# Residual, squares and norm statistic inside the first output projection, one expert's loads moved behind them, and three smaller moves, in a two-block network on one core

## The reference

```python
# first block
x = x + g1 * (jnp.concatenate([ssd_x, attn_x], axis=-1) @ w_out)
h2 = rms_norm(x, norm2) * (1 + sc2) + sh2
moe_x = hier_moe(h2, w_group, b_group, w_expert, b_expert, w_gate, w_up, w_down)
x = rms_norm(x + g2 * moe_x, norm_final)
# second block, two layers; xc (the context) goes the same way
merged = (g_f * (y_f @ w_br_fourier) + g_d * (o_d @ w_br_diff)
          + g_g * (o_g @ w_br_gqa) + g_c * (y_c @ w_br_conv))     # g_*: sigmoid gates
x = x + gx1 * rms_norm(merged @ w_out, g_post_mix)
hm = rms_norm(x, g_pre_mlp) * (1 + cx2) + sx2
x = x + gx2 * rms_norm(jnp.square(jax.nn.relu(hm @ w_ff1)) @ w_ff2, g_post_mlp)
```

## Time and profile before

| | before |
|---|---|
| median of 3 runs | 3932.5 us (3932.43 to 3933.34) |
| the profiled execution, its own time | 3933.81 us |
| its span in the trace | 3931.9 us |
| TensorE busy | 3729.5 us (95%) |
| VectorE busy | 1867.9 us (48%) |
| GpSimd busy | 1031.1 us (26%) |
| ScalarE busy | 832.4 us (21%) |
| mean granted clock of TensorE | 0.985 |
| DMA | 475.13 MB, mean 121 GB/s |

### The profile page before, as it was taken

One profiled execution on the slowest core, in us unless ns is written; L12 is line 12 of the kernel. 1 busy time (PEld: TensorE's weight loads), 2 busy tenths in 40 slices (PEclk: granted clock), 3 DMA queues, 4 the chain that ended last, 5 costly groups with the idle time before them and its releaser, 6 DMA issues. The chain is left out here.

```text
span 3931.9 us, 47902 instructions
## 1 busy us (share of the span) xinstructions
PE 3729.5 (95%) x18308; PEld 2555.2 (65%) x18308; DVE 1867.9 (48%) x3512; ACT 832.4 (21%) x1688; POOL 1031.1 (26%) x888
## 2 busy tenths in 40 slices
PE   7988789999999999999998999999999999989998
PEld 6776545555565586555554555555887767778887
DVE  4466323222412376886545666656125655143445
ACT  3125211111201264111213000002124611220001
POOL 2331100000023202132332222232142034443443
PEclk9999899999999999999999999999999999999999
DMA  5410599999411100222221222221120022212221
GB/s 213 187 71 1 220 351 395 394 395 398 195 59 54 38 1 17 93 89 77 102 79 54 108 107 107 107 87 53 49 76 23 12 75 81 81 65 97 86 86 54
DMA packets 72302, 475.13 MB, mean 121 GB/s; under 512 B 8272, under 2 KB 9680, under 8 KB 18960
## 3 DMA queue, kind: packets, MB, share of 16 engines
q1 hardware_dynamic: 68864, 461.35, 31.3%
q0 software_dynamic: 2640, 8.65, 0.8%
q10 hardware_dynamic: 576, 2.10, 0.1%
HBM read 467.87 MB, written 4.19 MB: 120 GB/s over the span
## 5 line engine op out<-in xcount | busy, mean ns | idle before, releaser
L1030 PE MATMUL ps<-projected,weight_ring 128*128 128x384 f32 (+1 forms) x672 | 245.8, 521 | 0.0
L3598 PE MATMUL ps<-projected,weight_ring 128*128 128x384 f32 (+1 forms) x768 | 223.0, 434 | 1.2 <-DVE mlp_u L3797 0.7
L2478 DVE SCALAR_TENSOR_TENSOR sb_x_all<-ps,sb_modulation_ada,sb_x_all 128x512 f32<-128x512 f32 x144 | 106.5, 750 | 244.6 <-PE ps L2303 215.0
L1030 PEld LDWEIGHTS ps<-projected,weight_ring 128*128 128x128 f32 x672 | 127.7, 190 | 106.1 <-issue 45.9
L3598 PEld LDWEIGHTS ps<-projected,weight_ring 128*128 128x128 f32 x768 | 144.8, 190 | 62.5 <-issue 3.0
L3598 PE MATMUL ps<-projected,mlp_weight_sums 128*128 128x384 f32 x480 | 165.8, 488 | 0.0
L1398 DVE TENSOR_REDUCE attention_shift<-ps 128x1 f32<-128x768 f32 (+1 forms) x160 | 130.9, 846 | 59.6 <-PE ps L1268 59.5
L2138 POOL DMA_INDIRECT h<-tokens,own_tokens x31 | 31.1, 1004 | 487.2 <-PE ps L2274 416.1
L3001 DVE SCALAR_TENSOR_TENSOR projected<-projected,sb_vectors 128x497 f32<-128x497 f32 (+26 forms) x270 | 157.9, 650 | 1.6
L3598 PE MATMUL ps<-h2b,weight_ring 128*128 128x384 f32 (+1 forms) x512 | 151.2, 439 | 6.5 <-ACT h2b L943 6.5
L2861 PE MATMUL ps<-projected,gate_sums 128*128 128x384 f32 (+1 forms) x512 | 151.1, 439 | 3.8 <-POOL gate_sums L3141 3.8
(11 more groups left out here) (670 smaller groups left out, 7697.6 us busy)
## 6 DMA issues: line engine op xcount, KB each, us to landing
weight_ring<-w_stream SPq DMA_DIRECT2D x217, 1024.0 KB, 5.0
expert_weights<-w_moe SPq DMA_DIRECT2D x125, 1024.0 KB, 23.0
weight_ring<-w_moe SPq DMA_DIRECT2D x40, 1024.0 KB, 23.3
h2b<-w_moe SPq DMA_DIRECT2D x33, 1024.0 KB, 23.1
weight_ring<-w_stream SPq DMA_DIRECT2D x16, 512.0 KB, 3.7
weight_ring<-w_stream SPq DMA_DIRECT2D x16, 384.0 KB, 3.2
sb_x_all<-xT SPq DMA_DIRECT2D x4, 768.0 KB, 7.2
tokens<-h_tokens ACTq DMA_DIRECT2D x4, 512.0 KB, 9.3
```

The costliest lines, as they stand in the source:

```text
L1030: ins = nc.tensor.matmul(core.ps[:, 2 * slot + half, 0:n], w_of(k), h_of(k)[:, a:a + n], start=(first and k == 0), stop=(last and k == chu ...
L2478: v.scalar_tensor_tensor(core.x[:, k, NCTX:T], ps[:, bank, :], core.mods["ada"][:, 40 + k, 1:2], core.x[:, k, NCTX:T], ALU.mult, ALU.add). ...
L3598: ins = nc.tensor.matmul(acc, wq[:, k, :], bq[:, k, :], start=(first and k == 0), stop=(last and k == 3), skip_group_check=True)
```

## The change

1. **`attention_phase(side=core.x)`**: before anything else in window attention, GpSimd makes the four weight sums of `project_out1`'s unit 0 (`side_quarters`) into the context columns of `core.x`, which nothing uses at that time. `project_out1` gets `made=1`: its GpSimd starts with unit 1.
2. **`ResidualTail`** in `project_out1`: each of the eight residual steps stands on VectorE behind the unit's own outputs, the first half behind `c12`, the second at the start of the next unit; ScalarE squares both halves at the start of the next unit, VectorE sums them, TensorE takes three ones-matmuls at the phase's end, ScalarE Ln and Exp. `residual_phase`, `rms_phase` and `modulate` are gone.
3. **`latent_norm_phase`** takes their place under the name `pre_moe`: six products with the statistic on VectorE and two on GpSimd, six scale-and-shift steps on ScalarE and two on VectorE.
4. **Loads**: `pre_moe` issues the routing weights and expert 0's six units; `ctx2T` and expert 1's six are issued at the start of `route_phase`.
5. **`gates_phase`**, both layers: in job 9 `statistic(acc, 0)` moves behind the second product into x, `statistic(acc, 1)` behind the second into z, VectorE's `mean_half(1)` behind `c12`.
6. **`mlp_phase`**: in both layers the third column sum is made after the first second-layer unit's `u2`; in layer 0, whose perceptron alone has mod units, `whole` also names the units 3, 11 and 19, the first behind a second-layer group's start.

```diff
-def rms_phase(core, name, src, chunks, col0, cols, finish, mods=(), loads=None):
-def modulate(core, name, src, dst, slot, shift, g, parts, mods=(), loads=None):
-def residual_phase(core, name, y, y0, gate):
+def latent_norm_phase(core, dst, rstd, slot, shift, g, loads):
+    pooled, vectored = (6, 7), (4, 5)
+    by_scalar = (0, 1, 6, 2, 3, 7)
...
         def _(sp):
             core.stream.load(sp)
+            loads(sp)
         def _(dve):
+            nc.vector.scalar_tensor_tensor(core.gain[:, slot, :, :], ...).then_inc(gain_ready, 1)
             for k in range(KD):
+                if k not in pooled:
+                    out, x = halves(k)
+                    nc.vector.tensor_tensor(out, x, rstd, ALU.mult).then_inc(normed, 1)
+            for k in vectored:
+                nc.vector.tensor_scalar(dst[:, k, :], dst[:, k, :], core.gain[:, slot, k, 1:2],
+                                        core.mod[:, shift + k, 1:2], ALU.mult, ALU.add)
...
+            for k in pooled:
+                nc.gpsimd.tensor_tensor(out, x, rstd, ALU.mult).then_inc(pooled_done, 1)
@@ route_phase, SyncE
             core.stream.load(sp)
+            sp.dma_start(core.x[:, :, 0:NCTX], core.aps["ctx2T"]).then_inc(st.ctx2_loaded, 16)
+            for u in range(6):
+                load_expert(core, st, sp, 1, u)
             sp.wait_ge(tokens_stored, 16 * XT)
@@ gates_phase, TensorE
                 product(z, s[:, 0], right(0, 1), True, False)
-                if j == TAPPED:
-                    if bg:
-                        pe.wait_ge(bg.added, bg.n_turn)
-                    pe.wait_ge(tapped, 1)
-                    statistic(acc, 0)
...
                 product(x, q.a12(w), right(4, 0), False, True)
+                if j == TAPPED:
+                    if bg:
+                        pe.wait_ge(bg.added, bg.n_turn)
+                    pe.wait_ge(tapped, 1)
+                    statistic(acc, 0)
@@ seven_phase, TensorE's end
+            if rt:
+                pe.wait_ge(c11_out, U - 1)
+                rt.total(pe, ps[:, 3 * (U % 2), :])
@@ seven_phase, ScalarE
                 f = units[i][3]
+                if rt and i >= 1:
+                    rt.square(act, i - 1)
...
+            if rt:
+                nc.scalar.preload_act_table_set(LOGS)
+                rt.square(act, U - 1)
+                rt.deviation(act, ps[:, 3 * (U % 2), :])
@@ seven_phase, VectorE
+                if rt and i >= 1:
+                    rt.residual(dve, i - 1, 1)
                 dve.wait_ge(products, 7 * i + 3)
                 dve.wait_ge(m1_out, i + 1)
                 plus(quarter(i, 0, 1), y, quarter(i, 1, 0), f).then_inc(u2_out, 1)
+                if rt and i >= 1:
+                    rt.add(dve, i - 1)
...
                 plus(quarter(i, 0, 1), z, quarter(i, 0, 1), f).then_inc(c12_out, 1)
+                if rt:
+                    rt.residual(dve, i, 0)
@@ ResidualTail
+    def square(self, act, n):
+        if n:
+            act.wait_ge(self.summed, n)
+        for r in range(2):
+            act.wait_ge(self.stayed, 2 * n + r + 1)
+            self.core.nc.scalar.activation(self.sq[r], two(self.core.x[:, 2 * n + r, NCTX:T]), ACT.Square) \
+                .then_inc(self.squared, 1)
@@ mlp_phase
-        whole = [i for i in range(len(mods)) if i == 0 or (i + 1) % (2 * U) == U - 1]
+        whole = [i for i in range(len(mods)) if i == 0 or (i + 1) % (2 * U) in (U - 1, U)]
...
                 v.tensor_tensor(t[:, 1], t[:, 0], b11, ALU.subtract).then_inc(ready, 1)
+                yield
                 v.tensor_tensor(t[:, 2], b21, t[:, 0], ALU.subtract).then_inc(ready, 1)
...
                 v.tensor_tensor(u2[:, p, :], y, m1[:, p, :], ALU.add).then_inc(u2_ready, 1)
+                if not up and j == 0:
+                    next(hid_sums)
@@ first_block, second_half
             seven_phase(core, "project_out1", cat, 0, NX // 2,
                         [(h[:, 2 * i, :], h[:, 2 * i + 1, :], False, 1.0) for i in range(4)],
-                        mods=mod_units("mod0", 2, 8), burst=2)
-            residual_phase(core, "residual1", h, NCTX, 16)
+                        mods=mod_units("mod0", 2, 8), burst=2, made=1, side=core.x,
+                        residual=(side[0], side[1:3], side[3], 16))
```

More of the change, by code:

```diff
@@ L1366, in _ @@
         def _(pool):
+            if side is not None:
+                side_quarters(pool, side, core.stream.arrived(pool, 0), side_ready)
             for p in range(N):
@@ L1461, in _, with halves @@
                                                    y_rstd[:, :], ALU.mult, ALU.mult)
-def residual_phase(core, name, y, y0, gate):
+def latent_norm_phase(core, dst, rstd, slot, shift, g, loads):
     nc = core.nc
-    with core.phase(name) as ph:
+    pooled, vectored = (6, 7), (4, 5)
+    by_scalar = (0, 1, 6, 2, 3, 7)
+    with core.phase("pre_moe") as ph:
+        gain_ready, normed, pooled_done = ph.sem("gain_ready"), ph.sem("normed"), ph.sem("normed_by_pool")
         block = ph.block()
+        def halves(k):
+            return two(dst[:, k, :]), two(core.x[:, k, NCTX:T])
         @block.sync
@@ L3281, in seven_phase @@
 def seven_phase(core, name, b, lo, n, units, th=None, conv=None, mods=(), burst=0, heads=None, tail=None,
-                sw=None, made=0, ahead=None, decay=None):
+                sw=None, made=0, ahead=None, decay=None, side=None, residual=None):
     nc, ps, stream = core.nc, core.ps, core.stream
@@ L3321, in seven_phase @@
         final = [(c11_out, c12_out), (c21_out, c22_out)]
+        rt = ResidualTail(core, ph, *residual, final, units) if residual else None
         contexts = np.cumsum([u[2] for u in units]).tolist()
@@ L3356, in _ @@
                 w = stream.take(pe).rearrange("p (k m) -> p k m", k=KD)
-                s = sw[:, i % 2]
+                s = [sw[:, i % 2, r] for r in range(4)]
+                if side is not None and i == 0:
+                    s = [SideQuarter(side, r) for r in range(4)]
                 x, y, z = banks(i)
@@ L3887, in first_block @@
     core.mod = core.mods["ada"]
+    side = [core.x[:, 2 * i:2 * i + 2, 0:NCTX] for i in range(4)]
     with ExitStack() as top:
```

217 lines of the change are left out of this document (98 added, 119 removed).

## The result

The changed kernel takes 3912.4 us (median of 5 runs, 3910.95 to 3917.95), the kernel before in the same comparison 3933.34 (3932.43 to 3938.41): a ratio of 0.9947, 95% interval 0.9935 to 0.996. That is 20.9 us less, where 18.0 less than the profiled execution was forecast, and 3912.4 for a predicted 3914.5. On a second chip the changed kernel took 3917.1 beside 3937.8 (experiment e11). The profiled execution took 3910.95, its span is 3909.1.

The account below looks back on a forecast made before the run. TensorE, busy nearly everywhere, was taken as the bound, so only its waits and lower clock could pay: 4.4 - 1.3 + 4.5 + 1.9 - 0.7 + 5.2 + 4.0 = 18.0 us off 3933.8, median 3914.5, range 3907 to 3921.

Parts of the forecast that it names:

- the first block: The parts from the first output projection through norm and routing to the experts, forecast to gain 7.6 us together.
- Sums of unit 0: First output projection: TensorE's two waits for GpSimd's weight sums go, at no cost in window attention; 4.4 us gained.
- Residual and squares inside: First output projection: the added steps make the m1 copy 0.4 us late in each of three units; 1.3 us lost.
- Norm: Between projection and routing: a shorter norm split over three engines lets the routing begin 11.5 us earlier.
- Stores and loads: Routing: token stores, issued earlier, share the queues with the backlog of loads and land 4.5 us earlier, not 11.5.
- Experts: Expert phase: moves as one piece at cost 0, since 7.5 us of idle weight stream can be given up.
- Gates: Gates phases: layer 0 gains 1.9 us as a wait of 3.30 goes; layer 1 loses 0.7.
- Perceptrons: Both perceptrons: waits for u2 go, whole mod units cost 2.6 us; 5.2 us gained in layer 0, 4.0 in layer 1.
- A: Routing: stores don't end last or overtake the loads; term at most 9.2 us, kernel at 3909.8; chance 0.12.
- B: Routing: stores get no more than before behind the load backlog; term 0, kernel at 3919.0; chance 0.13.
- C: Experts: weight stream loses its head start, adding waits and clock drops; kernel at 3947; chance 0.03.
- D: Gates and perceptrons: other waits replace those removed, gain of 13.0 gone; kernel at 3927.5; chance 0.05.

Follow-up runs that it names:

- e11: The changed kernel again, unedited, on a second chip; 3917.14 us, ratio 0.9952 to the kernel before.
- e1: Changed kernel with unit 0's weight sums made in the output projection again instead of window attention; 3915.98 us, one run.
- e8: Changed kernel with ScalarE's two squares of a unit moved behind the copies of m1 and m5; 3910.91 us, one run.
- e4: Changed kernel with GpSimd's two norm products given back to VectorE, ScalarE keeping six chunks in order; 3907.78 us, one run.
- e3: Changed kernel with all six of expert 1's loads issued only once the token stores have landed; 3913.75 us.
- e7: Changed kernel with the third column sum ahead of the second-layer group again, the whole mod units kept; 3912.63 us, one run.
- e6: Changed kernel with the gates' statistic back in both layers and mod units 3, 11 and 19 given back to VectorE; 3919.64 us, one run.
- e5: Changed kernel with expert 1's last three loads behind the token stores' landing, the first three ahead; 3908.78 us, ratio 0.9938 to the kernel before.
- e9: Changed kernel with expert 0's loads issued ahead of SyncE's wait for the routing weights in the norm phase; 3913.22 us.
- e10: Changed kernel with the edits of e4, e5, e8 and e9, and layer 1's gates statistic back where it was; 3907.31 us, ratio 0.9933.
- e2: Changed kernel with expert 1's six loads issued in the norm phase again, behind expert 0's; 3921.0 us, ratio 0.9972 to the kernel before.

## Why the prediction was right

The time, the range and the direction hold, and most steps do. That the sum comes within 2.1 us of the median is partly luck: the first block gave 2.8 less than forecast, gates and perceptrons 3.1 more, and 4.0 us between the medians stand in no stretch that the change touches. By its steps:

*Sums of unit 0.* 4.4 forecast; e1 gives 4.65. The cost in window attention is nothing, as taken. The first three sums took 2.24 to 2.27 us each in the projection of the kernel before, beside VectorE's column sums, and take 1.26 or 1.27 each where they are now.

*Residual and squares inside.* 1.3 lost was forecast; 0.9 was lost (e8), by the copy of `m1`, the cause named.

*Norm.* 11.5 forecast; the last output to the logits is 11.5 us in the changed kernel (438.8 to 450.3) where it was 23.0. GpSimd's share costs 0.94 instead of paying (e4). The Trainium skill ("SBUF — State Buffer", section "Who interferes with whom") says that a VectorE step with two inputs in SBUF and a GpSimd step that reads SBUF contend for a pair of ports that only one of them can hold. The trace agrees. In the 3.27 us in which both were at work VectorE lost 5.84 - 6 x 0.61 = 2.2, so it got 1.1 us of its own work done, and GpSimd 2 x 1.27 = 2.5: 3.6 in all in 3.3. With the factor of 1.8 of the prediction GpSimd's two steps would have taken 4.6 us. One after another the eight products are 6.2 us of work, where VectorE alone needs 4.9 for them (e4): the split could not win, and the rule was priced in the prediction as the side that speaks against it.

*Stores and loads.* A gain of 4.5 where the earlier issue alone would give 11.5: the backlog was to cost 7.0; it cost 8.1. (The working has a slip that the term of 4.5 hides: 474.5 and 14.5 us make 489.0, not 489.8, so that its own terms give 5.3. Measured are 3.5, that is 11.6 less 8.1.) The DMA queues of the changed kernel from 472 to 476 us, packets, MB and share:

```profile
q1 hardware_dynamic: 152, 1.11, 66.1%
q10 hardware_dynamic: 155, 0.54, 33.6%
```

Packet by packet in turn, as in the earlier trace rows, at 0.135 MB per us for the stores instead of 0.145. e3 takes the backlog away, and the stores land in 5.6 us.

*Experts.* The step that failed. The forecast let them move as one piece at no cost, with 7.5 us of idle stream to spare. Counted from the projection's start they do begin 7.2 us earlier in the changed kernel, for 7.6 forecast. But they took 2.46 us more there, in e11 3.3 more, and in the eight kernels with that order of loads 568.0 to 571.7 for 567.9, in the mean 2.2 more. From the projection's start to the matmul behind the experts the changed kernel, e11, e7 and e6, which share all code up to there, gained 4.8, 3.9, 5.7 and 3.2 on the kernel before, 4.4 in the mean, and not 7.6. The windows under e5 show part of it: granted clock 0.71 over the first 12 us, for 0.78 before, so 0.8 us of work less for the first expert, after TensorE had stood for 21.3 us instead of 13.4. Its first place comes free that much later: the first load of expert 3, which waits for TensorE's first products, goes out 8.1 us behind the experts' start for 7.2 before. That the stream therefore has less in hand at the end is argued and not shown. How the rest divides between the clock and the waits for weights, 4.9 to 10.0 us in the eight, isn't settled; with one profile of the kernel before it can't be told how much of it is that kernel's own spread.

The idle stream itself was real. It wasn't given up: it stands behind the experts' start in both kernels, 5.4 and 6.0 us, because the places are full until then. e5 gets it back, e3 moves it ahead of the start, and in e9 an earlier start of the stream alone brings no gain that shows.

*Gates.* 1.9 forecast in layer 0, as the middle between 2.7, if the clock holds behind the new wait, and 1.0, if it falls; 2.8 measured. Both ends came up: the clock held in the changed kernel and in e1 to e5, e7, e9 and e11 (462.3), and fell in e8 and e10 (464.0, a gain of 1.0). The new order alone doesn't decide which, and e6 shows that the old order can go without the drop as well. Layer 1 lost 0.77, for 0.7 forecast.

*Perceptrons.* 5.2 and 4.0 forecast, 6.3 and 5.1 measured. Drops of the clock in the first 60 us of these phases differ from run to run, so the moved sum is best counted from behind them, from the matmul behind the wait for L3797 (L3829 after; 0.7 us in layer 0, 0.5 in layer 1) to the phase's end:

| us, to the phase's end | before | changed | e11 | e6, sum moved alone | e7, whole units alone |
|---|---|---|---|---|---|
| layer 0 | 576.6 | 570.6 | 570.4 | 569.5 | 570.9 |
| layer 1 (no mod units) | 373.7 | 368.6 | 368.5 | 368.5 | 373.7 |

In layer 1 the four waits of 4.0 us in sum are worth 5.1. The forecast took them at their length; where the other 1.1 us comes from, no run shows. In layer 0 the moved sum alone gives 7.0, for 7.8 forecast, and the whole units alone 5.7; together they give 6.0. So the two edits remove the same waits (1.0 us of the 6.1 is left in e6, 0.3 in e7), and the units, once the sum has moved, cost 1.0 us on top. The forecast had 2.6 for them; with the 1.0 of waits that they still remove, their work on TensorE costs some 2.0, an estimate from these rows. So the 5.2 lies near the 6.0 because both of its parts were priced too high, and they have opposite signs.

*Rivals.* A is out: the stores were on the way for 18.8 us. B had the stores land no earlier against the projection's end; they land 3.5 earlier (11.6 gained before the logits, 8.1 lost behind them), so it fell as well. But what it gave the first block, 3.1, is nearer to the measured 4.4 than the forecast's 7.6, since the experts gave back part of what the routing had kept: the right size by the wrong mechanism. C names the right place with the wrong size: waits for weights of 4.9 to 10.0 us, with two drops of the clock among them at most. D fell.

## What to carry to other kernels

Ahead of a stage that streams weights into a fixed number of places, look at the stream's idle time and where it stands: an earlier start of the stage was worth here what it took from that (e3 against e5). A small transfer that releases the next stage should find little queued beside it, and a load that something waits for should go out ahead of the bulk (e2). And where two edits remove the same wait, take each out alone before both are kept: here the second cost 1.0 us on top of the first (e6, e7). Before two profiles are compared, look at the granted clock in both, stretch by stretch: what one drop costs is as much as what a small move brings.

## What the runs showed of the hardware

A VectorE and a GpSimd step that both read two tensors in the core's memory took turns: 3.6 us of work in 3.3 us, so that giving two of eight steps to GpSimd made the stage 0.94 us longer. SyncE's issues aren't free in depth: of twelve loads of 1 MB in a row each of the first ten took 0.33 to 0.67 us to issue, the eleventh 1.19 and the twelfth 2.11 (e2); in the changed kernel the first load behind `ctx2T`, with six others shortly ahead of it, took 6.97. TensorE's granted clock fell, mostly for 3.4 us at a time, in different places in kernels with the same code there: such a drop cost 1.4 us in window attention, 1.5 behind the statistic (e6 against the kernel before) and 1.7 in the projection behind the gates (75.09 for 73.39). Two profiles of one program, the changed kernel's and e11's, differ by 2.9 us in layer 1's perceptron for that reason alone.
